# Two-layer hybrid attention trunk: a buffer each for raw queries and raw keys, and an earlier eviction of the second query

## What is computed

```python
def trunk_layer(x, ...):
    h = rms_norm(x, norm1)
    a_q, a_k, a_v, b_q, b_k, b_v, i_q, i_k, i_w = split_cols(h @ w_in, PROJ_SPLITS)
    b_q = rms_norm(b_q.reshape(B, T, N_HEADS_B, HEAD_DIM), q_norm)
    b_k = rms_norm(b_k.reshape(B, T, N_HEADS_B, HEAD_DIM), k_norm)
    ...
    o_a = stick_breaking(a_q, ka, va, q_pos, k_pos)
    o_b = indexed_sparse_attention(b_q, kb, vb, i_q, ki, i_w, q_pos, k_pos, rel_bias, top_k)
    x = x + jnp.concatenate([o_a, o_b], axis=-1) @ w_out
    f, conv_new = conv_ffn(rms_norm(x, norm2), conv_state, w_up, conv_w, conv_b, w_down)
    return x + f, ...
```

## Time and profile before

| | |
|---|---|
| median of 3 runs | 1698.12 us |
| the runs | 1693.26 to 1698.87 us |
| the profiled execution's own time | 1691.3 us |
| its span in the trace | 1689.5 us |
| PE busy | 1591.6 us, 94% of the span |
| DVE, ACT, POOL busy | 57%, 40%, 37% |
| mean granted clock of TensorE | 0.979 of full |

### The profile page before, as it was taken

The page is one execution under the profiler, slowest core; times in us unless marked ns, Lnnn a source line. Parts: engine busy times, 40 slices in busy tenths (PEclk is TensorE's granted clock), DMA queues, the critical chain, the costliest instruction groups (busy, mean ns, idle before and its releaser), DMA issues.

```text
span 1689.5 us, 29872 instructions
## 1 busy us (share of the span) xinstructions
PE 1591.6 (94%) x11754; PEld 1471.0 (87%) x11762; DVE 966.1 (57%) x1764; ACT 683.6 (40%) x1296; POOL 631.2 (37%) x346
## 2 busy tenths in 40 slices
PE   6999998888999999999999999978899999999998
PEld 5788886766999999999987888766699999999998
DVE  6657666753666336616767667657365661663461
ACT  4335453543344224314433354534434431442342
POOL 5223331322733433433552333222255343334332
PEclk9999998988999999999999999999999999999999
DMA  6322210111333332233233222111123223323233
GB/s 186 91 82 84 70 39 25 52 45 46 88 87 89 88 88 81 84 95 90 72 86 116 82 69 57 40 43 46 53 63 88 82 83 96 88 81 88 86 88 94
DMA packets 242178, 131.43 MB, mean 78 GB/s; under 512 B 10302, under 2 KB 236590, under 8 KB 242038
## 3 DMA queue, kind: packets, MB, share of 16 engines
q1 hardware_dynamic: 242038, 129.52, 26.9%
HBM read 117.59 MB, written 11.62 MB: 76 GB/s over the span
## 4 chain that ended last, share of the span: by engine, by line
PE 72%; DVE 14%; ACT 6%; issue 3%; DVEq 3%; POOL 2%; ACTq 1%; DMA 0%; SPq 0%
PE g_ps L1168 13%; PE g_ps L1169 13%; PE g_ps L1172 13%; PE a_ps L1169 7%; PE a_ps L1172 7%; PE a_ps L1168 7%; PE a_ps L1261 2%; PE a_ps L1247 1%; POOL w_lo L1687 1%; DVE score L734 1%; PE a_ps L688 1%; DVE a_ps L1663 1%; ACT work L977 1%; DVE top L731 1%; DVE va L1481 1%
## 5 line engine op out<-in xcount | busy, mean ns | idle before, releaser
L1687 POOL TENSOR_TENSOR w_lo<-raw,w_hi 128x1024 fp32r<-128x1024 f32 (+2 forms) x210 | 504.6, 2403 | 710.7 <-ACT w_hi L884 710.7
L1168 PE MATMUL g_ps<-h_hi,w_hi 128*128 128x272 f32 (+1 forms) x1616 | 453.1, 298 | 14.7 <-DVEq L1570 8.8
L1169 PE MATMUL g_ps<-h_lo,w_hi 128*128 128x272 f32 (+1 forms) x1616 | 441.6, 292 | 0.0
L884 ACT ACTIVATE w_hi<-raw 128x1024 fp32r<-128x1024 f32 (+2 forms) x210 | 217.3, 1035 | 452.3 <-PE g_ps L1172 315.6
L1172 PE MATMUL g_ps<-h_hi,w_lo 128*128 128x272 f32 (+1 forms) x1616 | 338.6, 291 | 0.0
L1168 PEld LDWEIGHTS g_ps<-h_hi,w_hi 128*128 128x128 f32 (+1 forms) x1616 | 308.5, 191 | 28.8 <-DVEq L1570 10.7
L1169 PEld LDWEIGHTS g_ps<-h_lo,w_hi 128*128 128x128 f32 (+1 forms) x1616 | 308.4, 191 | 1.2 <-issue 0.5
L1579 DVE SCALAR_TENSOR_TENSOR wts<-work,par,wts 128x546 f32<-128x546 f32 x176 | 201.0, 1142 | 99.2 <-ACT wts L1061 92.1
L1172 PEld LDWEIGHTS g_ps<-h_hi,w_lo 128*128 128x128 f32 (+1 forms) x1616 | 255.9, 190 | 0.0
L1168 PE MATMUL a_ps<-h_hi,w_hi 128*128 128x272 f32 x720 | 194.4, 288 | 0.0
L1169 PE MATMUL a_ps<-h_lo,w_hi 128*128 128x272 f32 x720 | 194.3, 289 | 0.0
(11 more groups left out here) (234 smaller groups left out, 2795.8 us busy)
## 6 DMA issues: line engine op xcount, KB each, us to landing
raw<-in_w_up SPq DMA_DIRECT2D x88, 512.0 KB, 3.8
raw<-in_w_in SPq DMA_DIRECT2D x56, 512.0 KB, 3.8
raw<-in_w_down SPq DMA_DIRECT2D x32, 512.0 KB, 3.7
raw<-in_w_out SPq DMA_DIRECT2D x16, 512.0 KB, 3.8
raw<-in_w_down SPq DMA_DIRECT2D x16, 384.0 KB, 3.5
x_nat<-in_x_prompt SPq DMA_DIRECT2D x4, 512.0 KB, 6.4
strip<-bias_line SPq DMA_DIRECT2D x8, 256.0 KB
out_p_av<-v_nat SPq DMA_DIRECT2D x4, 512.0 KB, 5.6
```

What stands on the lines that cost most here:

```text
L884: act.activation(w_hi[:, n % SPLIT, 0:kt, 0:c], raw[:, n % RAW, 0:kt, 0:c], ACT.Copy).then_inc(hi_done, 1)
L1168: pe.matmul(g[0:c, a, 0:HALF], w_hi[:, s, j, 0:c], xh[:, mov], start=(j == 0), stop=False)
L1169: pe.matmul(g[0:c, a, 0:HALF], w_hi[:, s, j, 0:c], xl[:, mov], start=False, stop=False)
L1687: pool.tensor_tensor(w_lo[:, s, 0:kt, 0:c], raw[:, n % RAW, 0:kt, 0:c], w_hi[:, s, 0:kt, 0:c].bitcast(F32), ALU.subtract).then_inc(lo_done, 1)
```

## The change

It does two things. The raw keys of B get a buffer of their own: the last column of o_t in place of nraw. And in the list of steps the E of ("bq", 1) stands directly behind ASP, ahead of ASS and of the M and W of ("bk", 0), where it stood behind them. The S of ("bq", 1) stays where it was.

```diff
-    s += [("ASZ",), ("AW", 3), bq1[1], ("ASP",), ("ASS",), ("M", "bk", 0), ("W", "bk", 0), ("E", "bq", 1), ("S", "bq", 1), product("bk", 1)[0], ("ASV",)]
+    s += [("ASZ",), ("AW", 3), bq1[1], ("ASP",), ("E", "bq", 1), ("ASS",), ("M", "bk", 0), ("W", "bk", 0), ("S", "bq", 1), product("bk", 1)[0], ("ASV",)]
...
+        def norm_raw(kind):
+            return nraw[:] if kind == "bq" else o_t[:, KT - 1, :]
...
-                    act.activation(sq_slot(st), nraw[:], ACT.Square).then_inc(sq_done.sem, 1)
+                    act.activation(sq_slot(st), norm_raw(st[1]), ACT.Square).then_inc(sq_done.sem, 1)
...
-                        dve.scalar_tensor_tensor(q_t[:, q_slot("bq", p), :], nraw[:], qk_gain[:, 0:1], vb[:], ALU.mult, ALU.mult)
+                        dve.scalar_tensor_tensor(q_t[:, q_slot("bq", p), :], norm_raw("bq"), qk_gain[:, 0:1], vb[:], ALU.mult, ALU.mult)
...
-                        dve.scalar_tensor_tensor(k_t[:, k_slot("bk", p), :], nraw[:], qk_gain[:, 1:2], vb[:], ALU.mult, ALU.mult)
+                        dve.scalar_tensor_tensor(k_t[:, k_slot("bk", p), :], norm_raw("bk"), qk_gain[:, 1:2], vb[:], ALU.mult, ALU.mult)
...
-                        dve.tensor_tensor(halves(nraw[:]), g, halves(rstd[:]), ALU.mult)
+                        dve.tensor_tensor(halves(norm_raw(kind)), g, halves(rstd[:]), ALU.mult)
```

## The result

The changed kernel takes 1682.24 us (median of 6 runs, 1680.20 to 1688.00), the kernel before 1695.08 us (median of 6, 1693.26 to 1698.87). The ratio is 0.9925 with an interval of 0.9907 to 0.9944: 12.8 us faster, 0.75%. Two later series of the same kernel beside new runs of before gave 0.9920 (0.9904 to 0.9936) and 0.9937 (0.9925 to 0.9949). The profiled executions, 1691.3 and 1682.84 us, differ by 8.5.

A forecast was written before the change was run, and what follows sets the result against it. The prediction took PE to bound the kernel. Removing 2.90 us of idleness per layer, plus 4.4 us by the clock, gave 5.7 + 4.5 = 10.2 us; 1698.1 - 10.2 = 1687.9 us, range 1681 to 1696.

The forecast's parts named there:

- The buffer costs nothing: Squares, eviction and W of a key use another tile of the same shape, no instruction added; sum 0.
- The idleness goes in full: PE's wait between ASS and the half product of ("bk", 1) vanishes: 2.90 us per layer, 5.8 in all.
- What is late instead: M and W of ("bk", 0) come 0.72 to 0.9 us later on DVE; first case: POOL holds M's first operation, W's copy ends about 271.9.
- The clock stays up: PE keeps the full clock from ASS through the half product and ASV; gain 10.2 us, against 5.8 otherwise.
- The first BL starts 5.7 and 4.5 us earlier: Attention B's first BL starts at 275.75 instead of 281.45 in layer 0, 1104.1 instead of 1108.59 in layer 1.
- Nothing for attention B: Behind the first BL the ring moves as a whole; no gain taken, plus or minus 4.8 us kept for the range.
- The profiled execution at 1681.1: Whole kernel: the profiled 1691.3 us less the summed gain of 10.2 us.
- the way from the profiled execution to the median: Whole kernel: the median lies 6.8 us above the profiled execution, so 1698.1 - 10.2 = 1687.9.
- The price of the clock: In attention B, each microsecond at the lower level (1.2 GHz) costs 0.38 us, from its lengths in the two layers.
- only the idleness goes: Rival, 2 in 10: the lower level still comes in the passage or later in attention B; gain 5.8 us, time 1692.3.

The follow-up runs named there:

- half the move: Changed kernel, but the eviction of ("bq", 1) stands between M and W of ("bk", 0); 1689.70 us against 1693.48 for before.
- the filler: Kernel before plus 20 matmuls with unread results on PE between ASS and the half product of ("bk", 1); 1688.47 us against 1693.48, ratio 0.9976.
- a filler's profile: Changed kernel plus 28 matmuls with unread results on PE ahead of the third BL; 1681.80 us against the changed kernel's 1682.
- the early norm: Changed kernel with N, Y and M of ("bq", 1) moved ahead of ASV; 1680.07 and 1679.11 us in two series.
- fillers: Unread matmuls: 28 ahead of the changed kernel's third BL, 1681.80 us; 20 ahead of the second BL with the early norm, mean 1679.9 us.

## Why the prediction came out as it did

The forecast was 1687.9 with a range of 1681 to 1696; the median is 1682.2, inside it, at its lower edge. It lies outside the narrower range that belonged to the forecast itself, 1683 to 1693; what took it in were the 2 us added for the median of a few runs, and only 1.2 us of margin were left, so that it held is in part luck. By the steps:

- *The buffer costs nothing*: right, 1.0005 (0.9994 to 1.0015) by itself.
- *The idleness goes in full, 2.90 us in each layer*: right. The half product follows ASS without a gap in both layers, and half the move left 1.66 us.
- *What is late instead*: right, and of the two cases the first. The held operation is now the first of M, 2.66 us long beside POOL's 2.35; the eviction, from 265.20 to 265.90, was not held. W's copy ends at 271.58, 4.0 us ahead of the first BL. The Trainium skill, in "SBUF — State Buffer", section "Who interferes with whom", has the rule for it: a VectorE instruction with two SBUF inputs and a GpSimd instruction that reads SBUF exclude each other. The trace agrees: L1482 has two SBUF inputs and was held, the eviction has one in PSUM and ran on for 0.05 us beside POOL. That it is the operands, and not only which of the two started first, two other pairs of the changed kernel's profile show. In both the DVE operation starts inside the one of POOL. With one input in PSUM it takes its usual 0.72 us; with both in SBUF it ends 0.58 us behind POOL's and takes 0.99, where it takes 0.72 alone. The kind of operation is not it either, for before it was a TENSOR_TENSOR with both inputs in SBUF that was held for 2.79.

```profile
408.06 2.79 POOL L1690 TENSOR_TENSOR w_lo<-raw,w_hi 128x1024 fp32r<-128x1024 f32 x1 [18.06 <-ACT w_hi L887]
...
410.09 0.72 DVE L1559 TENSOR_TENSOR x_t<-x_t,g_ps 128x544 f32<-128x544 f32 x1 [1.48 <-PE g_ps L1175]
...
455.56 2.40 POOL L1690 TENSOR_TENSOR w_lo<-raw,w_hi 128x1024 fp32r<-128x1024 f32 x1 [2.31 <-ACT w_hi L887]
...
457.55 0.99 DVE L1482 SCALAR_TENSOR_TENSOR va<-va,vb 128x544 f32<-128x544 f32 x1 [1.48 <-ACT vb L923]
```

- *The clock stays up*: right, 1.00 through the passage in both layers of all three profiles of this kernel, and the filler shows the cause for the half product. ASV can have the lower level all the same, as one layer of a filler's profile shows.
- *The first BL starts 5.7 and 4.5 us earlier*: 281.45 - 275.60 = 5.85, of which 0.18 is an earlier start of ASS (265.32, before 265.50), so 5.7; in layer 1 it starts 1098.07 - 1087.77 = 10.30 us behind the start of ASS, and before it was 1108.59 - 1093.85 = 14.74 (1093.85 is from before's timeline), so 4.4.
- *Nothing for attention B*: 1.1 us shorter in layer 0, 0.6 longer in layer 1 in the profiled pair; right there, but by chance of the execution. From its first BL to its last product attention B takes 114.8 to 118.6 us in the six passages of the changed kernel's three profiles (mean 116.5) and 115.0 to 119.7 in the four of before and the buffer alone (mean 117.5).
- *The profiled execution at 1681.1*: it took 1682.84. The passages gave the 10.1 us, and attention B another 0.5, but by the start of layer 1's ASS 0.9 us of layer 0's gain were gone again (6.96 at the end of attention B, 1093.85 - 1087.77 = 6.08 there), and 1.5 behind attention B of layer 1. Both stretches differ from execution to execution: in the profiles of the seven other kernels and series without the early norm the one between the layers (from the last product of attention B to ASS) takes 692.8 to 693.9 us and the one behind layer 1's attention B 466.9 to 467.9. Before's profile, with 692.7 and 466.0, was the fastest in each, and the changed kernel's, with 693.6 and 467.5, is like the others. So most of these 2.4 us were before's luck in that profile and no loss of the change.

The mechanism was right; what was mis-sized is the last term, the way from the profiled execution to the median. I took 10.2 off the median of three runs, 1698.1. The error of 5.7 us has two parts: before's median of three was itself 3.0 us high (1695.08 with six runs; 1693.5 over the 49 later ones), and the change was worth 12.8 in this series, 11.5 over all, and not 10.2. At equal clock it gave 7.0 ± 1.0, where idleness alone says 5.8; by the clock 4.6, where I had 4.4 for the passages alone. The filler says the same without the line: 4.5 ± 1.7 by the clock, and 7.0 ± 1.9 from there to the changed kernel. The rest of some 1 us is within these errors, and stays open. The price of the clock, 0.38 us for each microsecond from the lengths of two attention Bs, came out as 0.29 over all runs. The rival "only the idleness goes" had it that the lower level would come back in the passage or in attention B; over 49 and 17 runs it did not, 16 us of it are gone.

The Trainium skill's rule that the monitor's phase is a matter of the run ("TensorE: Matmul & The Clock Gate", section "What's actually happening") is borne out: with the same order of instructions the long half product lay in layer 0 in one profile and in layer 1 in another, and runs of before have mean clocks from 0.975 to 0.982, and their times go with them. It moved the time from run to run, but did not take the gain away.

## What to carry to other kernels

Where PE is the bound and two units take turns in a PSUM slot, evict the older unit before any other work of the evicting engine, even at the price of a buffer: the wait costs itself, and then once more through the clock of the dense matmuls behind it. Test the second part with useless matmuls in the gap before believing it. The same clock is worth less where another engine sets the pace: there look how far a gain gets, link by link. And compare several profiles of each kernel before giving a microsecond a cause, since a lead won in one place can be lost two blocks later to the clock in one execution and kept in the next.

## What the runs showed of the hardware

- An idle time of PE of 1.66 us, behind thin matmuls, was followed by the lower level (clock 0.67 over the next 4.4 us); with 2.77 us of filler in 2.90 us of idleness the clock stayed at 1.00.
- The lower level also came with PE busy without a break: at the end of ASV in layer 1 of the filler kernel (clock 0.95 over ASV's 3.84 us, 0.50 over the 2.98 behind).
- The spread of this kernel's times, 1690.0 to 1698.9 for before, goes with the granted clock: 0.29 us for each microsecond at the lower level in 133 runs, with 1.4 us of scatter left. In dense stretches of PE the price was higher: 5.60 us of half product at the lower level against 3.1 at the full, 0.45 us for each, and 6.77 us at clock 0.56 against 4.01, 0.46 for each.
- 10 to 12 us less of the lower level in attention B, by fillers, made no difference to the time that the runs can tell (0.5 and 0.2 us, each ± 2.8).
- A DVE operation with both inputs in SBUF that starts inside one of POOL is held until that ends (2.66 us in place of 0.72 for L1482); one with an input in PSUM is not (L1559, 0.72 us inside POOL's 2.79).
